# A transformer kernel's setup stage interleaved with its first mixer, and rotary swaps taken from spare weight columns

## The reference, cut to what matters

```python
c_act = jax.nn.silu(c)
for l in range(DEPTH):                                   # DEPTH = 2
    mod = c_act @ ada_w[l] + ada_b[l]                    # 6 x 1024 columns
    sh_a, sc_a, g_a, sh_f, sc_f, g_f = jnp.split(mod, 6, axis=-1)
    h = modulate(rms_norm(x, attn_norm_g[l]), sh_a, sc_a)   # h * (1 + sc_a) + sh_a
    mix = hybrid_mixer(h, positions, w_in[l], ...)
    x = x + g_a[:, None, :] * mix
...
def hybrid_mixer(h, positions, w_in, q_norm_g, w_uq, ...):
    proj = h @ w_in
    c_q, c_kv, k_r, f_q, f_k, f_v, f_logit = jnp.split(proj, cuts, axis=-1)
    q = (rms_norm(c_q, q_norm_g) @ w_uq).reshape(B, S, 8, 64 + 32)
    q_rope = rope(q[..., 64:], positions)                # 32 columns of each head
    kv = (rms_norm(c_kv, kv_norm_g) @ w_ukv).reshape(B, S, 8, 64 + 64)
    k_rope = rope(k_r[:, :, None, :], positions)[:, :, 0, :]
    # two causal attentions of 8 heads, then two norms and @ w_o

def rope(x, positions):                                  # x1, x2: the two halves of x
    return jnp.concatenate([x1 * cos - x2 * sin, x1 * sin + x2 * cos], axis=-1)
```

## Time and profile before

| what | value |
|---|---|
| median of 3 runs | 2412.55 us (2411.41 to 2412.77) |
| profiled execution, its own time | 2411.62 us |
| its span | 2409.8 us |
| PE busy | 2223.1 us (92%) |
| DVE busy | 689.6 us (29%) |
| ACT busy | 319.3 us (13%) |
| DMA, mean over the span | 305 GB/s |
| granted TensorE clock, mean | 0.957 of full speed |

### The profile page before, as it was taken

One profiled execution on the slowest core, in us unless ns is written; L12 is line 12 of the kernel. 1 busy time (PEld: TensorE's weight loads), 2 busy tenths in 40 slices (PEclk: granted clock), 3 DMA queues, 4 the chain that ended last, 5 costly groups with the idle time before them and its releaser, 6 DMA issues. The chain is left out here.

```text
span 2409.8 us, 47351 instructions
## 1 busy us (share of the span) xinstructions
PE 2223.1 (92%) x21866; PEld 1356.5 (56%) x21866; DVE 689.6 (29%) x1274; ACT 319.3 (13%) x717; POOL 23.2 (1%) x21
## 2 busy tenths in 40 slices
PE   6999999999999999999999999899999997777776
PEld 5778888877734344353534444688789862221221
DVE  6763222336501101101101102455465431111111
ACT  2331000144200000000000000333232110000000
POOL 1000000000000000000000000000000000000000
PEclk9999999999999999999999999999999998877778
DMA  9658555701699999999999999433300579999998
GB/s 398 244 231 336 213 225 209 322 12 60 254 397 407 408 401 419 398 420 401 420 392 420 394 419 417 176 123 140 128 3 4 217 296 421 421 421 422 421 421 365
DMA packets 111472, 734.71 MB, mean 305 GB/s; under 512 B 12768, under 2 KB 16128, under 8 KB 36640
## 3 DMA queue, kind: packets, MB, share of 16 engines
q1 hardware_dynamic: 109328, 724.62, 74.2%
q0 software_dynamic: 1152, 4.19, 0.4%
q10 hardware_dynamic: 784, 2.75, 0.3%
HBM read 721.39 MB, written 10.09 MB: 304 GB/s over the span
## 5 line engine op out<-in xcount | busy, mean ns | idle before, releaser
L1558 PE MATMUL bank<-ring,moe_xg 128*32 128x512 f32 (+1 forms) x6144 | 581.0, 540 | 0.7 <-DVE moe_xg L1714 0.7
L1558 PEld LDWEIGHTS bank<-ring,moe_xg 128*32 128x32 f32 x6144 | 199.1, 110 | 377.3 <-issue 375.3
L1569 PE MATMUL bank<-ring,moe_turned 128*32 128x256 f32 x5376 | 291.5, 379 | 0.0
L1569 PEld LDWEIGHTS bank<-ring,moe_turned 128*32 128x32 f32 x5376 | 174.7, 110 | 117.1 <-issue 3.1
L1117 PE MATMUL bank<-h_chan,ring 128*128 128x256 f32 x896 | 195.6, 379 | 1.4 <-ACT h_chan L503 1.4
L1117 PEld LDWEIGHTS bank<-h_chan,ring 128*128 128x128 f32 x896 | 170.2, 190 | 24.7 <-issue 1.6
L2063 PE MATMUL bank<-ring,late 128*32 128x512 f32 x696 | 122.9, 806 | 51.8 <-DMA ring<-stream 51.8
L1753 DVE TENSOR_TENSOR moe_hidden<-moe_silu,bank 128x512 f32<-128x512 f32 (+1 forms) x48 | 26.9, 617 | 482.9 <-PE bank L1558 482.9
L2508 PE MATMUL bank<-h_chan,ring 128*128 128x256 f32 x672 | 148.0, 380 | 1.9 <-DVE h_chan L2613 1.9
L2508 PEld LDWEIGHTS bank<-h_chan,ring 128*128 128x128 f32 x672 | 127.0, 190 | 23.0 <-issue 6.3
L2063 PEld LDWEIGHTS bank<-ring,late 128*32 128x32 f32 x696 | 17.7, 122 | 150.2 <-DMA ring<-stream 129.8
(11 more groups left out here) (461 smaller groups left out, 2119.2 us busy)
## 6 DMA issues: line engine op xcount, KB each, us to landing
ring<-stream SPq DMA_DIRECT2D x257, 1024.0 KB, 22.7
ring<-wide SPq DMA_DIRECT2D x240, 1024.0 KB, 16.8
ring<-wide SPq DMA_DIRECT2D x128, 768.0 KB, 16.9
late<-stream SPq DMA_DIRECT2D x47, 1024.0 KB, 27.0
ada_slots<-stream SPq DMA_DIRECT2D x28, 1024.0 KB, 7.2
h_chan<-stream SPq DMA_DIRECT2D x9, 1024.0 KB, 26.7
rows<-zeros SPq DMA_DIRECT2D x8, 512.0 KB
moe_x_rows<-rows SPq DMA_DIRECT2D x28, 96.0 KB, 10.8
```

Of the source, the lines that this page charges most:

```text
L1558: mm = self.k.nc.tensor.matmul(banks[r][i * TILE:(i + 1) * TILE, 0:width], self.m.xg[:, r, t * TILE:(t + 1) * TILE], w[:, i, :], start=(t ...
L1569: mm = self.k.nc.tensor.matmul(self.sum_bank[r][q * TILE:(q + 1) * TILE, :], self.m.turned[:, r, n * TILE:(n + 1) * TILE], w[:, f2, q * T: ...
```

## The change

**Order of the modulation.** The first 8 slots of layer 0 are repacked: slot t now holds shift tile t and scale tile t, so that channel tile t of h can be finished when slot t is. Setup keeps slots 0 and 1 (`EARLY = 2`) and the norm; slots 2 to 7 are worked off inside the mixer's block, one between two tiles of h. The shift bias and the affine map of the amplitude go from two DVE instructions to three ACT instructions for each tile (two of 128 x 1, then the map of h itself with scale and shift). c and the product's scratch move from `hT` to ring place 13, and `hT` is free in setup.

**Order of the transfers.** x and `tab` are issued ahead of the modulation; three mixer slots go between modulation slots 1 and 2; `side` slots 0 to 2 come after mixer slot 5, and side slot 3 after mixer slot 9. `FIRST_ORDER` places the mixer's first two slots at 8 and 9, so that they need not wait.

**PE in mixer 0.** Items 0 to 5 are made together in six banks: for each channel tile of h, six matmuls, as that tile becomes ready. The latent sums follow, then items 6 and 7 and the rest as before.

**Rotation, both mixers.** The query weights have 128 columns a head, of which 96 were used; the 32 spare ones now hold a copy of the rotary columns with halves swapped, and `misc` has such a copy of k_r. The swapped values come out of the same matmul in rows 96 to 128, the sign lies in the sine's frequency table, and the five `turn` matmuls are gone.

```diff
+class FirstModulation:
+    EARLY, TILES = 2, 6
+    def dve(self, dve, slots, link):
+        dve_modulation(self.k, dve, self.loads, slots, 0, self.c_row, self.product, link,
+                       column=lambda t, i: DT * i + t)
+    def dve_tile(self, dve, t, link):
+        k = self.k
+        k.nc.vector.tensor_tensor(k.hT[:, t, :], k.xT[:, t, :], k.rstd[:, 0, :], ALU.mult)\
+            .then_inc(*k.counter("scaled").up())
+        if t >= self.EARLY:
+            self.dve(dve, [t], link)
+    def act_tile(self, act, t):
...
+        act.wait_ge(*self.loads.done(t))
+        a(shift, shift, ACT.Identity, bias=k.vec[:, bias + t:bias + t + 1]).then_inc(*ready.up())
+        a(scale, scale, ACT.Identity, scale=k.v("attn_g0", t), bias=amp).then_inc(*ready.up())
+        act.wait_ge(*ready.last())
+        act.wait_ge(*k.counter("scaled").at(t + 1))
+        a(k.hT[:, t, :], k.hT[:, t, :], ACT.Identity, scale=scale, bias=shift).then_inc(*k.counter("h_ready").up())
...
 stage_setup, SP:
-            for j in range(4):
+            sp.dma_start(k.xT[:, :, :], k.dram["xT"][:, :, :]).then_inc(*x_arrived.up(16))
+            sp.dma_start(k.tab[:, :], k.dram["tab"][:, :]).then_inc(*x_arrived.up(16))
+            for j in range(mod.EARLY):
                 loads.load(sp, j)
-            sp.dma_start(k.tab[:, :], k.dram["tab"][:, :]).then_inc(*x_arrived.up(16))
-            sp.dma_start(k.xT[:, :, :], k.dram["xT"][:, :, :]).then_inc(*x_arrived.up(16))
-            for j in range(4, loads.n):
+            for j in range(mod.TILES // 2):
+                nxt.load(sp, j)
+            for j in range(mod.EARLY, loads.n):
                 loads.load(sp, j)
...
-            nxt.load(sp, 0)
-            nxt.load(sp, 1)
-            side.head(sp)
...
-            keep_warm(k, k.bank[7], 32)
+            keep_warm(k, k.bank[7], 16)
...
 stage_mixer, SP (layer 0):
-                    for j in range(2, 10):
+                    for j in range(mod.TILES // 2, 6):
                         loads.load(sp, j)
-                    for j in range(side.slots, 2 * side.slots):
+                    for j in range(side.slots - 1):
+                        side.load(sp, j)
+                    for j in range(6, 10):
+                        loads.load(sp, j)
+                    for j in range(side.slots - 1, 2 * side.slots):
                         side.load(sp, j)
...
 stage_mixer, PE:
+                def joint_products():
+                    for t in range(DT):
+                        pe.wait_ge(*S("h_ready").at(t + 1))
+                        for n in range(joint):
+                            kind, j, i = items[n]
+                            w = slot_tiles(loads.ready(pe, j))
+                            mm = nc.tensor.matmul(bank_of(n)[:, 0:T], w[:, t, i * P:(i + 1) * P], k.hT[:, t, :],
+                                                  start=(t == 0), stop=(t == DT - 1))
...
-                            mm = nc.tensor.matmul(b[0:96, 0:T], w[:, t, i, 0:96], cq[:, t, :], start=(t == 0),
-                                                  stop=(t == 1))
+                            mm = nc.tensor.matmul(b[:, 0:T], w[:, t, i, :], cq[:, t, :], start=(t == 0), stop=(t == 1))
...
-                    if 27 <= n < 32:
-                        turn(n - 27)
...
 stage_mixer, DVE:
-                        link(v.tensor_tensor(turned, swapped, spread(sin[64:96, :], 2), ALU.mult))
+                        dve.wait_ge(*tile_out.at(10 + 2 * i))
+                        swapped, x = (qm[rows, 2 * i:2 * i + 2, :] for rows in (slice(96, 128), slice(64, 96)))
+                        link(v.tensor_tensor(turned, swapped, spread(sin[96:128, :], 2), ALU.mult))
...
+FIRST_ORDER = [8, 9, 0, 1, 2, 3, 4, 5, 6, 7, 10, 11, 12, 13]
```

More of the change, by code:

```diff
@@ L314, in keep_warm, with dve_modulation @@
         k.nc.tensor.matmul(bank[:, 0:P], ident, ident, start=True, stop=True)
-def dve_modulation(k, dve, loads, slots, l, c_row, product, link, first=0):
+def dve_modulation(k, dve, loads, slots, l, c_row, product, link, first=0, column=None):
     for j in slots:
@@ L655, in latent_sums @@
                     mm.then_inc(*lat_sum.up())
-                def turn(i):
-                    pe.wait_ge(*tile_out.at(10 + 2 * i if i < 4 else 4))
-                    if i >= 2:
-                        pe.wait_ge(*rope_ready.at(i - 1))
-                    src = qm[64:96, 2 * i:2 * i + 2, :] if i < 4 else misc[64:96, :]
-                    nc.tensor.matmul(rot_banks[i % 2][64:96, 0:512 if i < 4 else T], k.t("rot1")[64:96, 64:96], src,
-                                     start=True, stop=True).then_inc(*rot_done.up())
+                def joint_products():
[6 more added lines that the diff above has]
+                                                  start=(t == 0), stop=(t == DT - 1))
+                            if t == DT - 1:
+                                mm.then_inc(*((k.used, 1) if ends[n] else tile_done.up()))
                 keep_warm(k, k.bank[7], 10 if l else 5)
-                for n in range(len(items)):
+                if joint:
+                    joint_products()
+                    latent_sums()
+                for n in range(joint, len(items)):
                     if n == 8:
@@ L671, in _ @@
                     product(n)
-                    if n == 4:
+                    if n == 4 and not joint:
                         latent_sums()
-                    if 27 <= n < 32:
-                        turn(n - 27)
             @block.scalar
@@ L681, in _ @@
                     norm.act_root(act)
-                norm.act_shift(act, k.hT, k.mod[:, l, 0:8])
+                    norm.act_shift(act, k.hT, k.mod[:, l, 0:8])
+                else:
+                    for t in range(DT):
+                        mod.act_tile(act, t)
                 if side is not None:
@@ L733, in _ @@
                     norm.dve_inverse(dve, link)
-                norm.dve_scale(k.hT, k.amp[:, l, 0, :], norm.scaled)
+                    norm.dve_scale(k.hT, k.amp[:, l, 0, :], norm.scaled)
+                else:
+                    for t in range(DT):
+                        mod.dve_tile(dve, t, link)
                 dve.wait_ge(*S("small_arrived").at(16))
@@ L3326, in program @@
             if RUN is None or name in RUN:
-                loads[name] = Loads(k.weights, n, ring, turns, LAST_ORDER if name == "moe2" else None)
+                loads[name] = Loads(k.weights, n, ring, turns, {"moe2": LAST_ORDER, "mix0": FIRST_ORDER}.get(name))
                 if name == "ada":
@@ L3513 @@
     for l in range(2):
-        add(x["ada_w"][l].T.reshape(24, 2, P, D).transpose(0, 2, 1, 3).reshape(24, P, SLOT))
+        tiles = x["ada_w"][l].T.reshape(48, P, D)
+        if l == 0:
+            tiles = tiles[[DT * i + t for t in range(DT) for i in range(2)] + list(range(2 * DT, 48))]
+        add(tiles.reshape(24, 2, P, D).transpose(0, 2, 1, 3).reshape(24, P, SLOT))
     def mixer(l):
```

65 lines of the change are left out of this document (34 added, 31 removed).

## The result

| what | before | changed |
|---|---|---|
| median | 2412.66 us, 4 runs (2411.41 to 2412.94) | 2396.1 us, 4 runs (2394.92 to 2399.39) |
| profiled execution | 2411.62 us | 2399.39 us |
| its span | 2409.8 us | 2397.6 us |

The ratio is 0.9933, 95% interval [0.9921, 0.9946]: faster by 13 to 19 us, where 13.1 was forecast. The profiled execution, to which the sum was tied, gained 12.2 us (forecast 13.1); the median was lower than the forecast by 3.3 us, and lay outside the 2397 to 2402 that the prediction gave as likeliest, which the first experiment takes up.

A forecast was written before the change was run, and what follows sets the result against it. PE (780 us of experts) and transfers at 409 to 413 GB/s bound late stages, which move with the front. Gains 7.8 + 5.3 = 13.1 us turn profiled 2411.62 into 2398.5, median 2399.4; range 2395 to 2404.

The forecast's parts named there:

- likeliest: Whole kernel: the main case, forecast 2399.4 us, 2397 to 2402 with the spread of runs; chance 0.62.
- Transfers: Setup and mixer 0: slots land at 2.54 us a MiB, with 2.61 kept for the range.
- Most of the joint products' gain doesn't get through: Mixer 0: six items done at 45.8 instead of near 58.7, but queries start only 4.1 us earlier, at 61.4.
- Turns: Last eight items of each mixer: the five turn matmuls cost 5.3 us, more than their own busy time.
- Clock: Mixer 0, behind PE's longer pause before the queries: half a stretch of lowered clock charged, 1.7 us.
- slower by the clock: Rival: half clock from the joint products through queries, keys and values; block ends 21 us late, 2428 us; chance 0.03.
- Queries' width: Queries on PE: 128 columns for 96 only lengthen a weight load hidden beside the passes, costing nothing.
- Later stages: Experts and last stage: they begin earlier and keep their length, so time saved ahead reaches the end almost whole.
- The queue rival: Mixer 0: side slots 4 to 11 delayed, each of the last four 1 us late; 2403 us; chance 0.17.
- More is gained: Rival: fuller clock in attention and after, or faster transfers; 10 to 12 us in the first term, 2395 to 2397; chance 0.13.
- first term: Setup and mixer 0: the block ends near 104.5 instead of 112.25, 7.8 us earlier, bounds 6.0 to 9.6.
- The bound of 0.9 us between profile and median: Whole kernel: the median of the runs was taken as 0.9 us above the profiled execution.

The follow-up runs named there:

- E1: The first experiment: the changed kernel run again with no edit; median 2400.56 us, ratio 0.9955 to the kernel before.
- E6: Changed kernel with DVE's side slots 0 and 1 moved behind the latent norm; median 2399.67 us, ratio 0.9948 to the kernel before.
- E8: E6 and E7 together, side slots 4 and 5 issued between mixer slots 7 and 8, DVE's slots 6 to 11 spread among rotations; median 2394.28 us.
- E2: Kernel before with only the spare-column rotation, in both mixers; median 2399.03 us, ratio 0.9953 to the kernel before.
- E4: Changed kernel without joint products, PE's items one after the other as before; median 2405.93 us, ratio 0.9976 to the kernel before.
- E7: Changed kernel with side slot 3 issued ahead of mixer slots 6 to 9; median 2398.82 us, ratio 0.9944 to the kernel before.
- E12: E10 run again with no edit; median 2391.48 us, ratio 0.9914 to the kernel before.
- E9: Changed kernel with 28 unread matmuls in PE's pause ahead of mixer 0's queries; median 2398.19 us, ratio 0.9942 to the kernel before.
- E3: Changed kernel with the turns and permutation table put back, so setup, transfer order and joint products only; median 2408.14 us, ratio 0.9984 to the kernel before.
- E10: E11 with 14 unread matmuls behind PE's last item of mixer 0; median 2391.39 us, ratio 0.9924 to the kernel before.
- E11: E8 run again with no edit; median 2394.88 us, ratio 0.9929 to the kernel before.

## Why the prediction was right, by its steps

| step | forecast | changed kernel |
|---|---|---|
| root, inverse, barrier | 17, 19.2, 20 | 16.5, 18.5, 19.8 |
| modulation slot 2 lands | 24.8 | 23.9 |
| one slot and one tile of h | 2.97 | 2.87 |
| last slot done, joint products done | 42.2, 45.8 | 40.8, 45.0 |
| side slots 0 and 1 done | 54.4 | 54.4 |
| latents scaled, queries start | 61.4, 61.4 | 61.2, 61.30 |
| queries, keys, values with the clock | 13.1 + 1.7 | 14.92 |
| last eight items | 27.9 | 27.8 |
| side slot 3 lands | 67.1 | 66.7 |
| DVE, ACT end | 103.5, 104.5 | 103.1, 104.4 |
| first mixer, second mixer | 7.8, 5.3 | 7.8, 5.4 |

**Transfers.** 2.54 us a MiB, taken from a late stage, held as a mean from the first slot (11.66, after 3.07 MiB) to side slot 3 (66.70, after 24.7): the error is 0.4 us there. In between it was 2.45 up to slot 2, 2.63 from there to side slot 0 and 2.48 to side slot 3, so that side slot 0 came right (49.3) by two errors that cancel. By this the wait that mattered could be placed before anything had run. The early landing of slot 2 (0.9 us; in E1 it landed at 24.8, as forecast) and the shorter step made the joint products end 0.8 us early, and nobody was waiting for that.

**Most of the joint products' gain doesn't get through.** Right, with the reason named: six items complete 14 us earlier became 4.2 us at the queries. PE's pause was 7.28 us and not 5 to 6, since PE was done with items 6 and 7 at 54.0 and not at 55.5: 0.8 us of that is the earlier joint products, and the rest was put too high for the sums and two items, which took 9.1 us. The forecast left it there; E6 to E8 show what it did not work out: the order on DVE is worth nothing until side slots 3 to 5 come early too, and 5 to 7 us with them.

**Turns.** 5.3 us a mixer, worked out from the pace of undisturbed items, which is more than their busy time of 4.8. E2: 5.4 in the stretch itself, and 11.2 for both mixers at attention 1, of which some 0.5 belongs to the clock in attention (last section). The forecast's reason for the excess, that each turn empties the pipeline, was not tested by itself.

**Clock.** Forecast 1.7, measured 1.8 against the same stretch before (14.92 less 13.12), 2.3 in E1. Against full clock in that stretch it is 2.5: at full clock before, PE also waited a little for banks. The rival "slower by the clock" needed half clock in the joint products; it was 1.00 there. E4 lost it, with one item in place of six and a first pause of 4.56 us in place of 1.22, so the rival was a real one for narrower work.

**Queries' width.** 128 columns for 96 cost nothing, as forecast: 20 passes took 4.48 us before and in E2.

**Later stages.** They kept their lengths but for scatter: attention 1 was 13.3 us earlier, the span's end 12.2.

**The queue rival** (2403) asked for late side slots 4 to 11. From side slot 3's second product to its end at 103.1 DVE took 33.8 us, 33.9 forecast: no wait was added. **"More is gained"** (2395 to 2397) is where the first four runs fell, 2396.1. The marks show that its mechanism, a first term of 10 to 12 us by a fuller clock or faster transfers, did not occur (7.8 and 6.9); what put the median there was the scatter of the runs, and E1 gave 2400.6. The nine together (2397.7) lie 1.7 us below the forecast; with medians of one kernel 4.5 us apart, a closer agreement of one of them would have been luck, and it is the marks that bear the forecast out. The bound of 0.9 us between profile and median, taken from one execution, was too fine a term.

## What to carry to other kernels

A change at the front is a race between chains: list for each the last wait and when it ends, and expect nothing from an early chain until every other one is shortened too (E6 0.9 us, E7 0.3 us, both with slots 4 and 5 also early 5 to 7). Work that is fed piece by piece has to be wide enough that little of it is left behind the last piece, or the finer order costs more than it brings (here 5.4 us, E4). Where PE gets done early, fill the pause ahead of the next stage, counting float32 matmuls as two passes (2.3 us, E12), and look behind the mark as well: what the clock gives back in one place can be lost in the next pause (E9).

## What the runs showed of the hardware

**The same pause, two clocks.** Late in mixer 0's attention PE waits 1.7 us for DVE in every kernel. Timelines of PE, E3 and then the changed kernel:

```profile
136.91 0.66 PE L972 MATMUL bank<-tab_sb,score 128*128 128x128 f32 x4 [1.68 <-DVE score L1065]
...
138.09 1.38 PE L314 MATMUL bank<-tab_sb 128*128 128x128 f32 x10
```
```profile
130.89 1.01 PE L957 MATMUL bank<-tab_sb,score 128*128 128x128 f32 x4 [1.69 <-DVE score L1050]
...
132.88 2.12 PE L314 MATMUL bank<-tab_sb 128*128 128x128 f32 x10
```

Busy time by stretch, E3 and then the changed kernel:

```profile
138.00:140.00 2.00, 2.00 (x21) 1.74 (x19) 1.29 (x4) 0.69 (x3) 0.00 (x0) 1.00 0.00 0
```
```profile
131.00:133.00 2.00, 2.00 (x13) 1.34 (x13) 1.22 (x5) 1.70 (x8) 0.00 (x0) 0.51 0.01 4
```

The clock behind the pause was full (1.00) in the one and half (0.51) in the other. In 14 profiles the ten unread passes took 1.38 us four times (E3, E7, E9, E10) and 2.00 to 2.50 ten times. E10 and E12 are one kernel and fell on different sides. It is worth about 1.5 us up to the output projection (E12 against E10, the changed kernel against E3), and accounts for E3's larger lead at attention 1 (3.4 us) than at attention 0 (1.8). The Trainium skill, "TensorE: Matmul & The Clock Gate", part "What's actually happening", says that the number of matmuls at half rate at a kernel's start differs among its runs; these rows show such a difference behind a pause in the middle, where that page gives no number.

**Scatter in the middle.** From the first expert matmul of the 8-expert stage (out of `moe_xg`) to that of the last stage (out of `late`) the 14 profiles show 1312.6 to 1320.0 us, for one and the same kernel 1316.4 and 1320.0 (E11, E8); from there to the span's end it took 442 to 445. So the scatter lies chiefly ahead of the last stage, and not in it, as E1's expectation had it. What makes this scatter was not traced to its cause and stays open. It is larger than most effects of this study, which is why the marks, not the medians, decide them.
